# A decoder step on one Trainium2 core: the samples' attention moved into the first group's second gate-up stage of layer 0

## The chip, the core and the metric

The kernel runs on one core of one Trainium2 chip. A core has a matrix engine (TensorE, PE in the profile), a vector engine (VectorE, DVE), a scalar engine (ScalarE, ACT), a general engine (GpSimd, POOL) and a sync engine (SyncE, SP), which here issues all DMAs. The engines run their own instruction streams and meet at semaphores. The metric is device time in microseconds; lower is better.

## The reference

One inference step of a two-layer decoder for a prompt of 1024 tokens and for 8 samples of 8 new tokens each, with 512 cached positions per sample in pages. Layer 0 mixes by sparse attention (an indexer picks keys, then softmax attention over them) beside a pooling mixer; layer 1 by a gated spatial unit. Each layer ends in a SwiGLU feed-forward. Cut to the part that matters:

```python
def _dsa_block(q, iq, iw, qpos, k_all, v_all, ik_all, topk):
    rel = relu(einsum('bnhd,bsd->bnhs', iq, ik_all) * D_IDX ** -0.5)
    score = einsum('bnh,bnhs->bns', iw * N_IDX_HEADS ** -0.5, rel)     # masked to kpos <= qpos
    _, sel = lax.top_k(score, topk)
    k_sel, v_sel = take(k_all, sel), take(v_all, sel)
    logits = einsum('bnhgd,bnshd->bnhgs', qg, k_sel) * HEAD_DIM ** -0.5
    return einsum('bnhgs,bnshd->bnhgd', softmax(logits), v_sel)

def _swiglu(h, w_gu, w_down):
    gate, up = jnp.split(h @ w_gu, 2, axis=-1)
    return (jax.nn.silu(gate) * up) @ w_down

hs = hs + _rmsnorm(ms, norm_mix_post[layer])       # ms: mixer of the samples, with cached keys
hs = hs + _rmsnorm(_swiglu(_rmsnorm(hs, norm_ffn_pre[layer]), w_ffn_gate_up[layer], w_ffn_down[layer]), norm_ffn_post[layer])
```

## The kernel before, in words

The tokens are two groups: group 0 is prompt tokens 0 to 511, group 1 prompt tokens 512 to 1023 and the 64 sample tokens (width 576, done in two halves of 288). Activations stand transposed, eight blocks of 128 channels (`resid`, `mixed`). Every linear layer is cut into chunks of 128 output channels. Of a chunk, ACT makes the high part of the weights (`w_hi`), POOL the low part (`w_lo`), and PE does three products for each k-step (high by high, high by low, low by high). Two chunks are in flight, of the even chunks with PSUM banks 0 and 1, of the odd ones with 2 and 3. The feed-forward hidden size is done in two halves; one half is a gate-up stage (11 pairs of chunks, gate even and up odd, `Phase("gu", g, layer, half)`) and a down stage (`"dn"`).

The order of stages, written out by hand on each engine, is: input projections and indexers of both groups, attention of group 0, its output projection, gate-up and down of group 0 in layer 0 (halves 0 and 1), attention of group 1, the samples' attention (`attend_sample`), output projection of group 1, then layer 1 of group 0 and the rest. In the gate-up stages of group 0, DVE also does rounds of top-k for the large index tiles (`top_max`, `top_mark`), beside its two products (`TT` times the root, gate times up); ACT does `w_hi`, Silu and the copy to `hidden_split`; POOL does `w_lo`, one product and the low part of `hidden_split`.

The samples' attention in the kernel before: for each of eight samples PE transposes four pages of keys (line 1343), ACT copies them (1946), PE makes logits with the mask and the new keys (1375, 1376), DVE takes their minimum (2864), ACT the exponentials (1960), DVE divides (2866, 2869), PE transposes the probabilities (1350, 1351), ACT copies them (1951, 1952), PE multiplies with the values (1359, 1361). Everything has two buffers, and PE's order lets the steps of neighbouring samples overlap. SP loads the pages in four lots of eight (`key_value_pages`) during attention of group 1; then it loads back what was spilled: the residual of group 1 (`x_dram`), the residual and mixed rows of group 0 (`x0_dram`, `y0_dram`). These feed `hidden_update`, the end of group 0's layer 0, which runs under the output projection of group 1. SP's queue is in order: weights of the projection's chunks from 2 on are issued behind those loads.

Within the projection of group 1, six k-steps of chunk 0 are followed by a spread of the root (line 1075, `hidden_spread`), on which `hidden_update` waits.

## Time and profile before

| | us |
|---|---|
| median of 3 runs | 2657.81 (2653.18 to 2659.29) |
| the profiled execution | 2661.24 |
| its span | 2659.4 |
| PE busy in the span | 2541.2 (96%) |
| DVE / ACT / POOL busy | 1317.3 / 1027.7 / 1253.9 |

| stage (us of the span) | length |
|---|---|
| output projection, group 0 (412 to 456) | 43.6 |
| gate-up, group 0, layer 0, second half (652 to 772) | 119.8 |
| down behind it (772 to 832) | 60 |
| attention, group 1 (835 to 963) | 128 |
| samples' attention (963 to 999) | 36.6 |

PE is busy nearly all the time, so the chain that ends last is mostly PE's own; 79% of it is PE. A busy share does not say whether the matrix clock was full: that is the column PEclk, where 1.00 is 2.4 GHz and 0.50 is 1.2 GHz. A time line gives start and length of an instruction (or of a merged run of equal ones), and in brackets the idle time before it and who ended it. Ends of matmuls overlap the next starts, so lengths of steps are best taken from start to start.

### The profile page before, as it was taken

To read this page: it belongs to the slowest core of one execution; us is meant where nothing else is said; L and a number is where in the kernel's file an instruction comes from. 1 tells how busy PE (TensorE), PEld (TensorE's weight loads), DVE (VectorE), ACT (ScalarE), POOL (GpSimd) and SP (SyncE) were. 2 spreads that over 40 slices of the span, in tenths; PEclk is the share of its full clock that TensorE was granted. 3 is DMA by queue.
4 is the path that set the end of the run, shared out by engine and by line. 5 is a ranking of instruction groups with operands and counts; after the bars stand their busy time and mean duration, and the time that the engine had idled before them with its cause. 6 is when DMAs were issued, how large, how long until landed. Compare 5 with 4: busy or idle time off the path is not lost.

```text
span 2659.4 us, 42175 instructions
## 1 busy us (share of the span) xinstructions
PE 2541.2 (96%) x15118; PEld 2270.7 (85%) x15121; DVE 1317.3 (50%) x1705; ACT 1027.7 (39%) x1534; POOL 1253.9 (47%) x634
## 2 busy tenths in 40 slices
PE   6989869999998999999999999999999999999999
PEld 5779547888886769889999999888889999999999
DVE  4567777889877646554511233621344343220234
ACT  4545654422234645644422222532232435222222
POOL 4545243664665514535544443744543334443442
PEclk8989979999998999999999999999999999999999
DMA  6546012333333142332332232332343221232232
GB/s 154 129 105 154 16 60 64 103 104 93 95 105 113 43 146 68 123 104 87 112 92 70 83 86 72 96 105 85 95 134 119 72 81 43 86 89 75 81 94 68
DMA packets 451034, 246.41 MB, mean 93 GB/s; under 512 B 86668, under 2 KB 439648, under 8 KB 449383
## 3 DMA queue, kind: packets, MB, share of 16 engines
q1 hardware_dynamic: 450927, 244.99, 31.7%
q8 instruction: 66, 1.08, 0.2%
q14 instruction: 41, 0.34, 0.0%
HBM read 221.23 MB, written 23.82 MB: 92 GB/s over the span
## 4 chain that ended last, share of the span: by engine, by line
PE 79%; DVE 4%; ACT 3%; POOL 2%; issue 1%; DMA 1%; SPq 0%; DVEq 0%; POOLq 0%; ACTq 0%
PE psum L884 69%; PE psum L1306 1%; PE psum L1224 1%; PE psum L1328 1%; PE psum L1318 1%; POOL w_lo L2248 1%; DVE probs_t L2844 1%; PE psum L924 1%; PE psum L1049 1%; PE psum L1436 1%; ACT probs_t L1930 1%; PE psum L1075 0%; DVE row_stats L2830 0%; PE psum L1303 0%; DVE z_rows L3129 0%
## 5 line engine op out<-in xcount | busy, mean ns | idle before, releaser
L2248 POOL TENSOR_TENSOR w_lo<-w_raw,w_hi 128x1024 fp32r<-128x1024 f32 (+1 forms) x334 | 858.4, 2570 | 1133.8 <-ACT w_hi L1614 1115.0
L884 PE MATMUL psum<-act_split,w_hi 128*128 128x288 f32 (+1 forms) x5200 | 1049.6, 316 | 5.4 <-POOL w_lo L2248 5.3
L1614 ACT ACTIVATE w_hi<-w_raw 128x1024 fp32r<-128x1024 f32 (+1 forms) x332 | 372.9, 1123 | 1318.1 <-PE psum L884 1260.7
L884 PEld LDWEIGHTS psum<-act_split,w_hi 128*128 128x128 f32 x5200 | 808.2, 189 | 50.0 <-POOL w_lo L2248 5.8
L884 PE MATMUL psum<-act_split,w_lo 128*128 128x288 f32 (+1 forms) x2600 | 647.1, 315 | 0.0
L884 PE MATMUL psum<-hidden_split,w_hi 128*128 128x288 f32 (+1 forms) x2112 | 461.5, 327 | 0.5 <-POOL w_lo L2248 0.5
L884 PEld LDWEIGHTS psum<-act_split,w_lo 128*128 128x128 f32 x2600 | 433.7, 189 | 20.0
L884 PEld LDWEIGHTS psum<-hidden_split,w_hi 128*128 128x128 f32 x2112 | 339.4, 188 | 28.2 <-issue 0.9
L884 PE MATMUL psum<-act_split_first,w_hi 128*128 128x512 f32 x1088 | 340.1, 394 | 0.5 <-POOL w_lo L2248 0.3
L884 PE MATMUL psum<-hidden_split,w_lo 128*128 128x288 f32 (+1 forms) x1056 | 288.0, 327 | 0.0
L2964 DVE TENSOR_TENSOR temps<-psum,temps 128x512 f32<-128x512 f32 (+1 forms) x88 | 63.7, 724 | 358.5 <-PE psum L884 335.5
L884 PEld LDWEIGHTS psum<-act_split_first,w_hi 128*128 128x128 f32 x1088 | 203.6, 189 | 43.7 <-POOL w_lo L2248 1.1
L2956 DVE TENSOR_TENSOR temps<-psum,root_of_input 128x512 f32<-128x512 f32 (+1 forms) x88 | 63.7, 724 | 339.8 <-PE psum L884 332.2
L884 PE MATMUL psum<-act_split_first,w_lo 128*128 128x512 f32 x544 | 213.0, 392 | 0.0
L2478 DVE TENSOR_TENSOR square_sums<-square_sums,squares 128x512 f32<-128x512 f32 (+1 forms) x63 | 149.4, 2372 | 105.0 <-ACT squares L1979 60.9
L884 PEld LDWEIGHTS psum<-hidden_split,w_lo 128*128 128x128 f32 x1056 | 179.6, 188 | 13.8
L2967 DVE TENSOR_TENSOR hidden_split<-temps,hidden_split 128x576 f32 (+3 forms) x66 | 154.3, 2338 | 68.3 <-ACT hidden_split L1991 68.3
L2572 DVE MATCH_REPLACE8 scores<-top,scores 128x640 f32<-128x640 f32 (+3 forms) x192 | 170.0, 893 | 0.0
L2565 DVE MAX8 top<-scores 128x8 f32<-128x640 f32 (+3 forms) x192 | 164.7, 899 | 1.6
L2276 POOL TENSOR_TENSOR temps<-temps,root_of_input 128x512 f32<-128x512 f32 (+1 forms) x88 | 121.8, 1384 | 10.9 <-ACT temps L1988 10.9
L884 PEld LDWEIGHTS psum<-act_split_first,w_lo 128*128 128x128 f32 x544 | 102.7, 189 | 21.6
L1328 PE MATMUL psum<-probs_t,values_split 128*128 128x512 f32 x216 | 68.0, 425 | 17.8 <-DVE probs_t L2844 17.7
(334 smaller groups left out, 2452.9 us busy)
## 6 DMA issues: line engine op xcount, KB each, us to landing
w_raw<-in_w_ffn_gate_up SPq DMA_DIRECT2D x352, 256.0 KB, 3.2
w_raw<-in_w_ffn_down SPq DMA_DIRECT2D x64, 384.0 KB, 3.6
w_raw<-in_w_ffn_down SPq DMA_DIRECT2D x64, 320.0 KB, 4.0
w_raw<-in_w_in_odd SPq DMA_DIRECT2D x64, 256.0 KB, 3.0
w_raw<-in_w_in_even SPq DMA_DIRECT2D x60, 256.0 KB, 3.9
w_raw<-in_w_out_odd SPq DMA_DIRECT2D x32, 256.0 KB, 3.2
x_rows<-in_x_prompt SPq DMA_DIRECT2D x8, 512.0 KB, 6.0
w_raw<-in_w_out_even SPq DMA_DIRECT2D x32, 128.0 KB, 3.0
```

What stands on the lines that cost most here:

```text
L884: mm = pe.matmul(PS[:, 2 * p + b, 0:hi - lo], w[:, p, at], x(k)[:, lo:hi], start=(k == order[0] and w is WH and x is x_hi), stop=(k == ord ...
L924: mm = pe.matmul(PS[:, 2 * p + b, 0:hi - lo], w[:, p, at], x(k)[:, lo:hi], start=(k == 0 and w is WH and x is a_hi), stop=(k == ph.kt - 1 ...
L1328: mm = pe.matmul(PS[:, 6 + z, :], VS[:, v, kk, :], PT[:, kc % 2, q, :], start=kk == 0 and v == 0 and q == 0, stop=kk == t and v == 1)
L1614: act.activation(WH[:, p, 0:n], WR[:, p, 0:n], ACT.Copy).then_inc(S("w_hi"), 1)
L2248: pool.tensor_tensor(WL[:, p, 0:n], WR[:, p, 0:n], WH[:, p, 0:n].bitcast(F32), ALU.subtract).then_inc(S("w_lo"), 1)
L2276: pool.tensor_tensor(TT[:, 0, 0:T[g]], TT[:, 0, 0:T[g]], RB[g][:, 0:T[g]], ALU.mult).then_inc(S("gated"), 1)
L2478: dve.tensor_tensor(SS[:, 0:T[g]], SS[:, 0:T[g]], SQ[:, p, 0:T[g]], ALU.add).then_inc(S("ss_p"), 1)
L2565: ins_ = dve.max(M8[0:s.shape[0], m, :], s)
L2572: ins_ = dve.match_replace(out=s, in_to_replace=M8[0:s.shape[0], m, :], in_values=s, imm_value=CHOSEN)
L2956: dve.tensor_tensor(hv(TT[:, 0, 0:T[g]], g), lin(0, g), hv(RB[g][:, 0:T[g]], g), ALU.mult).then_inc(S("free_d0"), 1)
L2964: dve.tensor_tensor(hv(TT[:, 1, 0:T[g]], g), lin(1, g), hv(TT[:, 0, 0:T[g]], g), ALU.mult).then_inc(S("free_d1"), 1)
L2967: dve.tensor_tensor(flat(HR[:, 1, ds(i, 1), 0:T[g]]), TT[:, 1, 0:T[g]], flat(HR[:, 0, ds(i, 1), 0:T[g]].bitcast(F32)), ALU.subtract).then_ ...
```

## The change

The samples' attention leaves its place behind attention of group 1 and is done in pieces within gate-up of group 0, half 1, of layer 0. That stage is now written out (no loop) for its 22 chunks. Sample b has: transposes of its key pages in chunk 2b ahead of k-step 4, logits in chunk 2b+1 ahead of k-step 4, transposes of the probabilities in chunk 2b+3 ahead of k-step 3, values in chunk 2b+4 ahead of k-step 6. ACT's and DVE's parts follow their own work for a chunk (`sample_aside`, `sample_guest`). Key copy, probabilities and their transposes have one buffer instead of two; transposed keys and transposed probabilities share PSUM bank 6, logits use banks 4 and 5, the outputs bank 7. The pages lie where the residual `X` was (it is spilled then), and SP issues the four pages of keys and values of sample b between the weights of that stage. The queries of the samples are loaded in the first attention; the mask is made by DVE ahead of the first down stage, the heads are laid out by ACT behind it. The loads of spilled rows change place: the residual and six of eight mixed blocks of group 0 once the last prompt logits are made, the last two mixed blocks and the residual of group 1 once the last prompt values are done.

```diff
-        XH = over("resid_spare", [P, NB, T[0]], F32, h_at, 4096)
-        YH = over("mixed_spare", [P, NB, T[0]], F32, h_at, 8192)
-        SQH = over("squares_spare", [P, 2, T[0]], F32, h_at, 0)
+        XH = over("resid_spare", [P, NB, T[0]], F32, h_at, 0)
+        YH = over("mixed_spare", [P, 6, T[0]], F32, h_at, 9600)
+        YT = over("mixed_spare_tail", [P, 2, T[0]], F32, h_at, 7168)
+        SQH = over("squares_spare", [P, 2, T[0]], F32, h_at, 4096)
...
+        KP = over("key_pages", [P, 2, NPG, P], F32, x_at, 0)
+        VP = over("value_pages", [P, 4, NPG, P], F32, x_at, 1024)
+        KTB = over("page_keys_t", [P, PAST], F32, x_at, 3072)
+        PTS = over("probs_sample_t", [P, 5 * NS], F32, x_at, 3584)
+        PRS = over("probs_sample", [NS, KCOL], F32, x_at, 3904)
+        QZ = over("queries_sample", [P, DB, NS], F32, ikt_at, 0)
+        MKS = over("mask_sample", [NS, KCOL], BF16, ikt_at, 512)
+        QS = over("queries_sample_rows", [P, 4, NS], F32, ikt_at, 800)
...
+            def pages(b):
+
+                if b > 1:
+                    sp.wait_ge(S("kt_ps"), b - 1)
+                if b > 3:
+                    sp.wait_ge(S("pvs_mm"), b - 3)
+                for i in range(NPG):
+                    page = sp.value_load(PGT[0:1, NPG * b + i:NPG * b + i + 1], min_val=0, max_val=DB * NPG * 5 // 4 - 1)
+                    for to, name in ((KP[:, b % 2, i, :], "cache_k"), (VP[:, b % 4, i, :], "cache_v")):
+                        rows = ins[name][0].rearrange("n s h d -> n s (h d)")[ds(page, 1)].rearrange("a s d -> (a s) d")
+                        sp.dma_start(to, rows).then_inc(S(f"pages_in{b % 2}"), 16)
...
+                    sp.dma_start(QS[:], q_dram[1, :, :, 512:T[1]]).then_inc(S("qs_in"), 16)
...
                     next_queries(g, k)
                 if g:
-                    key_value_pages(0)
-                    sp.wait_ge(S("mk"), 6)
-                    key_value_pages(1)
-                    sp.wait_ge(S("qst_lo"), 16)
-                    sp.dma_start(QR[:, :, 0:NS], q_dram[1, :, :, 512:T[1]]).then_inc(S("q_in"), 16)
-                    key_value_pages(2)
-                    sp.wait_ge(S("p_tr"), kbase(7, 1))
-                    key_value_pages(3)
-                    sp.wait_ge(S("p_tr"), kbase(8, 0))
-                    sp.dma_start(X[:], x_dram).then_inc(S("first_in"), 16)
+                    sp.wait_ge(S("qk_mm"), 64)
+                    sp.dma_start(XH[:], x0_dram).then_inc(S("first_in"), 16)
+                    sp.dma_start(YH[:], y0_dram[:, 0:6, :]).then_inc(S("first_in"), 16)
                     sp.wait_ge(S("pv_mm"), kbase(8, 0))
-                    sp.dma_start(XH[:], x0_dram).then_inc(S("first_in"), 16)
-                    sp.wait_ge(S("pvs_mm"), 2)
-                    sp.dma_start(YH[:], y0_dram).then_inc(S("first_in"), 16)
+                    sp.dma_start(YT[:], y0_dram[:, 6:8, :]).then_inc(S("tail_in"), 16)
+                    sp.dma_start(X[:], x_dram).then_inc(S("second_in"), 16)
...
-            channel(0, 0, (1,))
+            ph = phase("gu", 0, 0, 1)
+            head(ph)
+            pages(0)
+            for i in range(1, FH):
+                some(ph, i, i + 1)
+                if i < DB:
+                    pages(i)
+            head(phase("dn", 0, 0, 1))
+            rest(phase("dn", 0, 0, 1))
...
+            def sample_keys(b):
+                pe.wait_ge(S(f"pages_in{b % 2}"), 128 * (b // 2 + 1))
+                wait(pe, S("ktb"), b)
+                wait(pe, S("pts"), b - 1)
+                for j in range(NPG):
+                    mm = pe.transpose(PS[:, 6, P * j:P * j + P], KP[:, b % 2, j, :], IDENT)
+                mm.then_inc(S("kt_ps"), 1)
+
+            def sample_logits(b):
+                pe.wait_ge(S("ktb"), b + 1)
+                pe.wait_ge(S("iqz"), 3)
+                pe.wait_ge(S("qz0"), 3)
+                wait(pe, S("exps"), b)
+                for bank, lo, hi, keys in ((4, 0, PAST, KTB[:]), (5, PAST, KCOL, KT[:, SEQ:SEQ + NS])):
+                    pe.matmul(PS[0:NS, bank, 0:hi - lo], EB[:, b, :], MKS[:, lo:hi], start=True, stop=False)
+                    mm = pe.matmul(PS[0:NS, bank, 0:hi - lo], QZ[:, b, :], keys, start=False, stop=True)
+                mm.then_inc(S("qks_mm"), 1)
+
+            def sample_turn(b):
+                pe.wait_ge(S("ps_norm"), 2 * b + 2)
+                pe.wait_ge(S("ktb"), min(b + 2, DB))
+                wait(pe, S("pts"), b)
+                for j in range(NPG):
+                    pe.transpose(PS[:, 6, NS * j:NS * j + NS], PRS[:, P * j:P * j + P], IDENT[0:NS, 0:NS])
+                pe.transpose(PS[0:NS, 6, NS * NPG:NS * NPG + NS], PRS[:, PAST:KCOL], IDENT[0:NS, 0:NS]).then_inc(S("ps_tr"), 1)
+
+            def sample_values(b):
+                pe.wait_ge(S("pts"), b + 1)
+                for j in range(NPG):
+                    pe.matmul(PS[:, 7, NS * b:NS * b + NS], VP[:, b % 4, j, :], PTS[:, NS * j:NS * j + NS],
+                              start=j == 0, stop=False)
+                pe.matmul(PS[:, 7, NS * b:NS * b + NS], VN[0:NS, 8, :], PTS[0:NS, NS * NPG:NS * NPG + NS],
+                          start=False, stop=True).then_inc(S("pvs_mm"), 1)
...
-            gate_up(phase("gu", 0, 0, 1))
+            sample = {}
+            for b in range(DB):
+                sample[2 * b, 4] = lambda b=b: sample_keys(b)
+                sample[2 * b + 1, 4] = lambda b=b: sample_logits(b)
+                sample[2 * b + 3, 3] = lambda b=b: sample_turn(b)
+                sample[2 * b + 4, 6] = lambda b=b: sample_values(b)
+            gate_up(phase("gu", 0, 0, 1), sample, FH)
             down(phase("dn", 0, 0, 1))
             attend(1)
-            attend_sample()
...
+            def page_keys(b):
+                act.wait_ge(S("kt_ps"), b + 1)
+                wait(act, S("qks_mm"), b)
+                act.activation(KTB[:], PS[:, 6, :], ACT.Copy).then_inc(S("ktb"), 1)
+
+            def sample_turned(b):
+                act.wait_ge(S("ps_tr"), b + 1)
+                wait(act, S("pvs_mm"), b)
+                act.activation(PTS[:, 0:NS * NPG], PS[:, 6, 0:NS * NPG], ACT.Copy)
+                act.activation(PTS[0:NS, NS * NPG:NS * NPG + NS], PS[0:NS, 6, NS * NPG:NS * NPG + NS], ACT.Copy).then_inc(S("pts"), 1)
+
+            def sample_exponentials(b):
+                act.wait_ge(S("mxs"), b + 1)
+                wait(act, S("ps_tr"), b)
+                act.activation(PRS[:], PSF[0:NS, 2048:2048 + KCOL], ACT.Exp,
+                               bias=MX[0:NS, 0, b:b + 1], scale=-1.0, accum_out=MX[0:NS, 2, b:b + 1]).then_inc(S("exps"), 1)
+
+            def sample_aside(c):
+                b, odd = divmod(c, 2)
+                if odd == 0 and b < DB:
+                    page_keys(b)
+                if odd and 1 <= b <= DB:
+                    sample_turned(b - 1)
+                if odd and b < DB:
+                    sample_exponentials(b)
...
-            gate_up(phase("gu", 0, 0, 1))
+            for j in range(4):
+                heads_of_sample(j)
+            gate_up(phase("gu", 0, 0, 1), False, sample_aside, FH)
...
+            def sample_mask():
+
+                dve.memset(QZ[:], 0.0).then_inc(S("qz0"), 1)
+                dve.wait_ge(S("top"), 2 * (SMALL + 17))
+                dve.tensor_scalar(MKS[:], SCS[:, 0:KCOL], SPLITTER, MASK, ALU.is_gt, ALU.mult).then_inc(S("qz0"), 1)
+
+            def sample_guest(c):
+                b, odd = divmod(c, 2)
+                if odd and b < DB:
                     dve.wait_ge(S("qks_mm"), b + 1)
-                    dve.tensor_reduce(MX[0:NS, 0, b:b + 1], PSF[0:NS, 1024 * (b % 2):1024 * (b % 2) + KCOL], AX.X, ALU.min).then_inc(S("mx"), 1)
+                    dve.tensor_reduce(MX[0:NS, 0, b:b + 1], PSF[0:NS, 2048:2048 + KCOL], AX.X, ALU.min).then_inc(S("mxs"), 1)
+                if odd == 0 and 1 <= b <= DB:
+                    b -= 1
                     dve.wait_ge(S("exps"), b + 1)
-                    dve.reciprocal(MX[0:NS, 3, b:b + 1], MX[0:NS, 2, b:b + 1]).then_inc(S("inv"), 1)
-                    dve.wait_ge(S("inv"), 64 + b + 1)
-                    pr = PRS[:, b % 2, :]
-                    dve.tensor_scalar(pr, pr, MX[0:NS, 3, b:b + 1], None, ALU.mult).then_inc(S("ps_norm"), 1)
-                dve.wait_ge(S("o_hi"), 17)
-                for half in range(2):
-                    r = slice(64 * half, 64 * half + 64)
-                    for j in range(4):
-                        at = AR[r, 0, j, 512:T[1]].rearrange("p (b t) -> p b t", b=DB)
-                        lo = AR[r, 1, j, 512:T[1]].rearrange("p (b t) -> p b t", b=DB)
-                        ins_ = dve.tensor_tensor(lo, PS[r, 7, :].rearrange("p (b h t) -> p h b t", b=DB, h=8)[:, 4 * half + j],
-                                                 at.bitcast(F32), ALU.subtract)
-                ins_.then_inc(S("o_lo"), 1)
+                    dve.reciprocal(MX[0:NS, 3, b:b + 1], MX[0:NS, 2, b:b + 1]).then_inc(S("ps_norm"), 1)
+                    dve.wait_ge(S("ps_norm"), 2 * b + 1)
+                    dve.tensor_scalar(PRS[:], PRS[:], MX[0:NS, 3, b:b + 1], None, ALU.mult).then_inc(S("ps_norm"), 1)
...
                     if (g, s) == (1, 0):
-                        dve.wait_ge(S("first_in"), 48)
+                        dve.wait_ge(S("second_in"), 16)
                     if (g, s) == (0, 1):
-                        dve.wait_ge(S("first_in"), 48)
+                        dve.wait_ge(S("first_in"), 32)
                     if (g, s) == (0, 2):
-                        dve.wait_ge(S("first_in"), 80)
+                        dve.wait_ge(S("first_in"), 64)
                 else:
                     dve.wait_ge(S("x_new"), m + n)
+                    if (g, s) == (0, 1) and n == 6:
+                        dve.wait_ge(S("tail_in"), 16)
...
             gate_up(phase("gu", 0, 0, 0), BIG0)
+            sample_mask()
             down(phase("dn", 0, 0, 0), 1, (2, 2, 2, 1), BIG0 + FH)
-            gate_up(phase("gu", 0, 0, 1), BIG0 + FH + 7)
+            gate_up(phase("gu", 0, 0, 1), BIG0 + FH + 7, None, sample_guest)
```

On PE, inside that gate-up stage: before, a chunk is a loop's body of products only.

```order
L1004 UNCONDITIONAL_BRANCH
L1004 ISA
L876 REGISTER_ALU
L884 MATMUL psum<-act_split,w_hi 128x512 x2
L884 MATMUL psum<-act_split,w_lo 128x512
L884 MATMUL psum<-act_split,w_hi 128x512 x2
```

After (chunk 3: the end of its k-step 2, then the probabilities of sample 0, k-step 3, the logits of sample 1, k-step 4):

```order
L888 MATMUL psum<-act_split,w_hi 128x512 x2
L888 MATMUL psum<-act_split,w_lo 128x512
L1363 MATMUL psum<-constants,probs_sample 128x64 x4
L1364 MATMUL psum<-constants,probs_sample 64x64
L888 MATMUL psum<-act_split,w_hi 128x512 x2
L888 MATMUL psum<-act_split,w_lo 128x512
L1354 MATMUL psum<-mask_sample,spread_bf_78 64x512
L1355 MATMUL psum<-page_keys_t,queries_sample 64x512
L1354 MATMUL psum<-mask_sample,spread_bf_78 64x64
L1355 MATMUL psum<-keys_t,queries_sample 64x64
L888 MATMUL psum<-act_split,w_hi 128x512 x2
L888 MATMUL psum<-act_split,w_lo 128x512
```

The small products of two samples now stand between k-steps of one chunk.

On ACT, in the same stage, the loop's body before:

```order
L1614 ACTIVATE w_hi<-w_raw 128x1024
L173 REGISTER_ALU
L1988 ACTIVATE temps<-temps 128x512
L173 REGISTER_ALU
L1614 ACTIVATE w_hi<-w_raw 128x1024
L1991 ISA
L1991 ACTIVATE hidden_split<-temps 128x512
```

After (from the end of chunk 1, where sample 0's exponentials are, over chunk 2 to chunk 3):

```order
L1984 ACTIVATE hidden_split<-temps 128x512
L1946 ACT_TABLE_LOAD
L1946 ACTIVATE probs_sample,row_stats<-psum,row_stats 64x576
L1607 ACTIVATE w_hi<-w_raw 128x1024
L1981 ACT_TABLE_LOAD
L1981 ACTIVATE temps<-temps 128x512
L1935 ACTIVATE page_keys_t<-psum 128x512
L1607 ACTIVATE w_hi<-w_raw 128x1024
L1984 ACTIVATE hidden_split<-temps 128x512
L1940 ACTIVATE probs_sample_t<-psum 128x256
L1941 ACTIVATE probs_sample_t<-psum 64x64
```

Keys' copies, probabilities' copies and exponentials have come in, and a table load stands ahead of each exponential and ahead of the Silu (`temps<-temps`) behind it.

On SP, at the end of attention of group 1, before (the last page of keys and values, the spilled rows, then the projection's weights):

```order
L676 DMA key_pages_139<-in_cache_k 128x128
L676 REGISTER_ALU
L676 DMA value_pages_140<-in_cache_v 128x128
L672 REGISTER_ALU
L672 COMPARE_AND_BRANCH
L711 DMA resid<-resid_spill 128x4608
L713 DMA resid_spare<-resid_spill_first 128x4096
L715 DMA mixed_spare<-mixed_spill_first 128x4096
L585 UNCONDITIONAL_BRANCH
L585 ISA
L536 ISA
L536 DMA w_raw<-in_w_out_even 64x4x128
```

After:

```order
L702 DMA act_split<-pool_spill 128x2304
L692 DMA queries_tile<-queries_spill 128x4x128 x2
L707 DMA resid_spare<-resid_spill_first 128x4096
L708 DMA mixed_spare<-mixed_spill_first 128x3072
L710 DMA mixed_spare_tail<-mixed_spill_first 128x1024
L711 DMA resid<-resid_spill 128x4608
L584 UNCONDITIONAL_BRANCH
L584 ISA
L535 ISA
L535 DMA w_raw<-in_w_out_even 64x4x128
```

The pages are gone from here, and the residual stands last ahead of the weights.

## Rows read from the trace of the kernel before

**Rows 1.** Windows: us, busy of PE, PEld, DVE, ACT, POOL, PEclk, DMA.
```profile
412.25:455.80 43.55, 43.55 (x196) 36.04 (x194) 36.55 (x57) 14.94 (x22) 16.79 (x7) 1.00 0.27 76
652.40:772.20 119.80, 119.80 (x530) 99.26 (x529) 96.51 (x148) 35.18 (x45) 79.55 (x43) 1.00 0.32 95
962.60:999.20 36.60, 34.73 (x201) 22.59 (x199) 12.00 (x25) 15.42 (x41) 0.00 (x0) 0.92 0.63 213
```

**Rows 2.** PE's timeline (start us, us, what): samples' attention, then the projection.
```profile
962.63 1.03 PE L1343 MATMUL psum<-constants,key_pages 128*128 128x128 f32 x8
...
972.86 0.66 PE L1343 MATMUL psum<-constants,key_pages 128*128 128x128 f32 x4
...
976.88 0.66 PE L1343 MATMUL psum<-constants,key_pages 128*128 128x128 f32 x4
...
999.24 1.33 PE L884 MATMUL psum<-act_split,w_hi 128*128 128x288 f32 x4
...
1005.98 1.06 PE L1075 MATMUL psum<-constants,root_rstd 128*128 128x128 f32 x8
```

**Rows 3.** PE's timeline: chunk 1 and its k-step 3 in gate-up.
```profile
657.85 0.61 PE L884 MATMUL psum<-act_split,w_hi 128*128 128x512 f32 x2
...
659.89 0.62 PE L884 MATMUL psum<-act_split,w_hi 128*128 128x512 f32 x2
```

**Rows 4.** ACT's timeline behind chunk 0 of gate-up.
```profile
658.24 1.06 ACT L1614 ACTIVATE w_hi<-w_raw 128x1024 fp32r<-128x1024 f32 x1 [4.00 <-PE psum L884]
659.20 0.61 ACT L1988 ACTIVATE temps<-temps 128x512 f32<-128x512 f32 x1
```

**Rows 5.** ACT's timeline in layer 1: table load between w_hi and Gelu.
```profile
1133.90 1.06 ACT L1614 ACTIVATE w_hi<-w_raw 128x1024 fp32r<-128x1024 f32 x1 [1.21 <-PE psum L884]
1134.98 1.28 ACT L2134 ACT_TABLE_LOAD   x1
1136.27 0.63 ACT L2134 ACTIVATE u_t<-u_t 128x512 f32<-128x512 f32 x1
```

**Rows 6.** ACT's timeline: keys' copy; w_hi of the projection's chunk 2.
```profile
973.55 0.60 ACT L1946 ACTIVATE page_keys_t<-psum 128x512 f32<-128x512 f32 x1
...
1012.17 1.04 ACT L1614 ACTIVATE w_hi<-w_raw 128x1024 fp32r<-128x1024 f32 x1
```

**Rows 7.** PE's timeline: gaps inside dense work and what follows.
```profile
1217.62 1.06 PE L1014 MATMUL psum<-constants,square_sums 128*128 128x1 f32 x8 [1.08 <-DVE square_sums L2885]
1218.54 1.31 PE L884 MATMUL psum<-act_split,w_hi 128*128 128x288 f32 x4
...
1222.51 0.69 PE L884 MATMUL psum<-act_split,w_hi 128*128 128x288 f32 x4
...
2110.27 1.16 PE L1436 MATMUL psum<-w_spatial_t,z_rows 128*128 128x128 f32 x8 [1.99 <-DVE z_rows L3129]
...
2111.72 0.80 PE L884 MATMUL psum<-act_split,w_hi 128*128 128x288 f32 x4
...
2112.61 0.69 PE L884 MATMUL psum<-act_split,w_hi 128*128 128x288 f32 x4
...
2113.40 0.69 PE L884 MATMUL psum<-act_split,w_hi 128*128 128x288 f32 x4
```

**Rows 8.** Window behind the gap at 1217; columns as in rows 1.
```profile
1219.00:1220.00 1.00, 1.00 (x6) 1.00 (x6) 0.10 (x1) 1.00 (x1) 0.00 (x0) 0.50 1.13 337
```

**Rows 9.** SP's timeline: two page issues of the old stage.
```profile
897.75 0.36 SPq L676 DMA_DIRECT2D key_pages<-in_cache_k  x1
...
899.77 0.36 SPq L676 DMA_DIRECT2D key_pages<-in_cache_k  x1
```

**Rows 10.** The DMA view: what, count, KB each, median us to landing.
```profile
resid<-resid_spill SPq DMA_DIRECT2D x1, 2304.0 KB, 9.4
...
w_raw<-in_w_out_even SPq DMA_DIRECT2D x16, 256.0 KB, 3.1
```

**Rows 11.** PE's timeline: chunk 2 of the projection starts.
```profile
1015.77 0.80 PE L884 MATMUL psum<-act_split,w_hi 128*128 128x288 f32 x4 [0.75 <-POOL w_lo L2248]
```

166 lines of the change are left out of this document (46 added, 120 removed).

## The prediction

> **What bounds the kernel now.** I read the windows by stage first. In the stage that takes the moved work, 652.4 to 772.2 us, PE is busy all of the 119.8 us while DVE is busy 96.5, POOL 79.6 and ACT 35.2 [rows 1]: TensorE alone sets the pace. In the samples' attention, 962.6 to 999.2, PE is busy 34.7 of 36.6 us, with ACT at 15.4 and DVE at 12.0 [rows 1]. So the work that is moved is itself TensorE work, and it goes to a stage where TensorE has no room. The move can win only what is not PE's work: the start and end of the old stage, and whatever the low clock cost there. Next I read PE's own timeline for the sizes, then ACT's, because PE will wait for ACT in the new place.
>
> **What is removed.** The old stage starts at 962.63 and the output projection behind it at 999.24 [rows 2]: 36.6 us leave the path. The projection then ran its first six k-steps in 1005.98 - 999.24 = 6.74 us [rows 2]. A k-step of this width takes 2113.40 - 2112.61 = 0.79 at full clock [rows 7], six take 4.8. In the new kernel the projection follows the prompt's attention directly. The same succession exists already in the first group, whose projection runs at a granted clock of 1.00 throughout, 412 to 456 us [rows 1]. I therefore take 6.74 - 4.8 = 1.9 us more as won. Together -38.5 us.
>
> **What PE gets in gate-up.** One sample costs PE 976.88 - 972.86 = 4.02 us in the old steady state (page transposes, logits, probability transposes, values) [rows 2]; eight are 32.2 us. They stand in 32 groups (turn of keys, logits, turn of probabilities, values) between wide products, and the first wide pair behind small ones starts late: between 0 and 0.1 us each, since a k-step right behind small products takes 2112.61 - 2111.72 = 0.89 where the usual one takes 0.79 [rows 7]. I take near half, 1.4 us for 32: +33.6, bounds 32.2 and 35.4.
>
> **The wait that PE gets.** PS bank 6 holds in turn the transposed keys and the transposed probabilities. So the turn of sample b's probabilities, in chunk 2b+3 ahead of k-step 3, waits for ACT's copy of the keys of sample b+1, which ACT makes behind chunk 2b+2. Count from the start of chunk 2b+3. PE is at k-step 3 after 659.89 - 657.85 = 2.04 us [rows 3]. ACT starts w_hi at 658.24 - 657.85 = 0.39, and Silu at 1.35 [rows 4]. In the changed kernel Exp and Silu alternate on ACT, and the order shows an ACT_TABLE_LOAD ahead of every Exp and of every Silu behind one, 16 in all; none stands in this stage before. Where such a load stands between w_hi and its function, it starts 1134.98 - 1133.90 = 1.08 after w_hi starts and the function 1136.27 - 1134.98 = 1.29 later [rows 5]. So: w_hi 0.39, load 1.47, Silu 2.76, keys' copy about 0.52 later (instructions on ACT overlap by some 0.1) at 3.28, its 0.60 [rows 6] to 3.88, PE some 0.1 later: 3.98. PE waits 3.98 - 2.04 = 1.94 us. This holds for b = 0 to 6 (for b = 7 there is no next key copy): 7 x 1.94 = +13.6 us. Without the loads it would be 0.5 each. Queued behind the waiting turn is all of PE's remaining chunk; nothing hides it. The Exp's own load falls behind an odd chunk, whose followers are due a whole chunk later, and costs nothing.
>
> The Trainium skill, "ScalarE: Activation LUTs", section "Table sets: the hidden batching unit", says to batch calls by table set, which speaks against this change. Its section "What ACT_TABLE_LOAD costs" puts a switch at 1.28 us plus 1.38 of drain. The rows show 1.28 and no drain: w_hi ends at 1134.96, the load starts at 1134.98 [rows 5]. By the page the wait would be 3.3 us and the sum about 9.7 us more.
>
> **What the wait does to the clock.** In the linear stages the trace has four gaps of PE of 1.08 to 1.99 us inside dense work (the shortest and the longest stand; the other two are of the same kind) [rows 7]. Behind three of them, the shortest among these, the granted clock is 0.50, the 1.2 GHz level, for some 3.5 us, as in 1219 to 1220 [rows 8]; behind the longest the k-steps still come at 0.79. A fall costs 1222.51 - 1218.54 = 3.97 for three k-steps of 0.79, so 1.6 us [rows 7]. Three in four of seven gaps is five: +8.0 us, bounds 0 and 11.2. The small products right behind each gap are why I don't go lower.
>
> **The other engines.** DVE gets at most the old stage's 12.0 us [rows 1] on 96.5 in a stage that grows past 160 us; its scaling of the probabilities is queued before the long top-k instructions and is done before ACT's copy. ACT gets 15.4 + 16 x 1.28 = 36 on 35.2, again far from full; POOL gets nothing. They cost nothing because PE's own work covers them; were DVE late, PE's turn would wait for it instead. SP issues four pages a sample at 899.77 - 897.75 = 2.0 us each [rows 9], 8 us within a period of 15, ahead of weights that are due a chunk and more later: taken as 0, bound +1 us. The queries' small load in the first attention and the mask made ahead of the down stage: 0, as DVE has several us there before its next product.
>
> **The projection's weights.** The residual (2304 KB) and two blocks of the mixed rows (512 KB) are now issued at about 962.9, when the attention that ended at 962.63 [rows 2] has its last values, and the weights of chunk 2 behind them; before, the whole samples' stage lay between the loads and their use. The residual takes 9.4 us to land [rows 10]; 512 KB more are between 0 and 2.1 us by its rate, I take 1.2; then the weights, between 0 and the 3.1 of their own row [rows 10], I take 1.5: 962.9 + 9.4 + 1.2 + 1.5 = 975.0. ACT would want them 1012.17 - 1005.98 = 6.2 us after the spread starts [rows 2, 6], in the new kernel at 962.63 + 4.8 + 6.2 = 973.6. So about 1.4 us late, 1.7 with the delay of the issue itself, on top of the 0.75 that PE waits there anyway [rows 11]: +1.7, bounds 0 and 5 (with a fall of the clock behind it). The loads of the first group's residual and most of its mixed rows are issued after the last logits product and have the last value rounds to land in: 0. Taking the heads' copies out of the last rounds of attention gains 0 to 0.5; I take 0.
>
> **Sum.** -38.5 + 33.6 + 13.6 + 8.0 + 1.7 = +18.4 us on the profiled execution of 2661.24. The median of the runs shown is 3.4 lower, 2657.81, so 2676.2 us (0.7% slower). With the bounds: +7.6 (no fall, no late start, weights 0.3 late) to +26.7, 2665 to 2685.
>
> **Rivals.**
> 1. *PE does not wait, or hardly.* If the key copy comes in time (the load overlapped with PE's chunk in a way that the rows don't show), neither wait nor fall of the clock arises: -38.5 + 33.6 + 1.7 = -3.2, 2654.6, and 2651.5 with the lowest bounds. It is on the other side. The point is whether the copy ends within 2.04 us of the chunk's start; for it only that the loads carry no wait of their own, against it that ACT executes in order and has w_hi, load, Silu ahead. 0.15, of which 0.06 below -0.2%.
> 2. *A load costs more than its row*, as the skill's page has it; worked with a further stop as long as w_hi (1.06) ahead of each load, 7 x 1.06 = 7.4 us more, 2684. 0.06.
> 3. *Pages or weights come late.* If SP's page issues push the weights of gate-up past their use, each pair of chunks loses a few tenths to 1 us, 8 in all, 2684; for it that SP is in order, against it that eight page issues take 8 us of each 15 and the weights' own issues 1 to 2. 0.05.
> 4. *The clock stays low through the stage's middle*, because gap, turn and logits follow closely: every chunk then costs twice 5.44; two such chunks more are 11 us, 2687 and up. 0.06.
> The forecast's own case keeps 0.68. That the work is not moved is excluded by the order.
>
> **How the numbers follow.** A measurement of this kernel tells about 0.2%, 5.3 us, from no change. Slower by more: 0.68 + 0.06 + 0.05 + 0.06 less a little where the forecast's gaps are short, 0.82. Within: 0.11. Faster: 0.07. The range 2662 to 2686 holds the forecast's bounds and most of rivals 2 and 3, and leaves out rival 1 and the far end of 4.
>
> **What would show it.** In gate-up: eight periods of about 17 us for two chunks, seven PE gaps near 1.9 us at the turn of probabilities released by ACT's page_keys_t, table loads of 1.28 between w_hi and Silu, clock 0.5 behind most gaps, the stage 170 to 178 us long. In the projection: clock 1.00 and one gap of 2 to 3 us for w_lo at chunk 2. I am wrong if the gaps are half a microsecond, or if the clock holds.

## The result and the profile after

| | before | after |
|---|---|---|
| median of 6 runs each, us | 2657.97 (2652.08 to 2659.38) | 2671.56 (2666.58 to 2672.73) |
| profiled execution / its span, us | 2661.24 / 2659.4 | 2672.57 / 2670.8 |

The changed kernel is slower: ratio 1.0054, 95% interval 1.0040 to 1.0067, 13.6 us between the medians and 11.3 between the profiled executions. The forecast had +18.4, 2676.2 in a range of 2662 to 2686. Direction and mechanism of the wait hold; the size is 4.6 us too large.

First the windows by stage of the kernel after. Columns as in rows 1: length, busy time of PE, PEld, DVE, ACT and POOL, the granted clock, the DMA share, GB/s.

```profile
653.20:822.10 168.90, 157.87 (x729) 118.94 (x729) 107.90 (x180) 73.17 (x117) 78.97 (x43) 0.99 0.32 92
677.00:678.00 1.00, 1.00 (x3) 0.52 (x2) 0.77 (x1) 0.00 (x0) 0.57 (x1) 0.50 0.25 63
...
1012.10:1070.50 58.40, 55.85 (x410) 55.37 (x409) 38.11 (x35) 31.38 (x50) 29.67 (x15) 0.97 0.44 131
```

The first row answers to the second of rows 1: the gate-up stage has grown from 119.8 to 168.9 us, and PE is busy in 157.9 of them. So 11 us of the growth is PE standing still, which it never did in this stage before. The second row is one microsecond with the clock at 0.50; the third is the projection of group 1.

The length of each part of the span, from the first product of one stage to the first of the next:

| part | before | after | difference | forecast |
|---|---|---|---|---|
| up to gate-up (group 0, layer 0, second half) | 652.41 | 653.25 | +0.8 | 0 |
| gate-up with the samples' groups | 119.68 | 168.92 | +49.2 | +55.2 |
| down, attention of group 1, (before) samples' attention | 227.15 | 190.01 | -37.1 | -36.6 |
| projection of group 1 | 57.46 | 58.36 | +0.9 | -0.2 |
| from there to the end | 1602.7 | 1600.3 | -2.4 | 0 |

I don't put the last line and the first down to the change. The last part takes 1596.8 to 1604.1 us in the traces of all kernels below, and 1600.3 and 1604.1 in two executions of the same changed kernel. Some of it is the clock: the kernel before has stretches of 0.50 at 1218 and at 1648 (some 1.7 us lost in each) that the kernel after lacks, but the kernel after has one at 1076 and one at 2124 that the kernel before lacks.

PE's timeline after, the first product of each of the eight turns of the probabilities; in brackets the idle time before it and what ended it:

```profile
676.39 0.43 PE L1363 MATMUL psum<-constants,probs_sample 64*128 64x64 f32 x4 [1.63 <-ACT page_keys_t L1935]
...
694.94 0.43 PE L1363 MATMUL psum<-constants,probs_sample 64*128 64x64 f32 x4 [1.57 <-issue]
...
711.96 0.43 PE L1363 MATMUL psum<-constants,probs_sample 64*128 64x64 f32 x4 [1.57 <-issue]
...
728.99 0.43 PE L1363 MATMUL psum<-constants,probs_sample 64*128 64x64 f32 x4 [1.57 <-issue]
...
794.97 0.46 PE L1363 MATMUL psum<-constants,probs_sample 64*128 64x64 f32 x4
```

Seven gaps, one for each sample but the last, 17.02 us from turn to turn (711.96 to 728.99); only the first period has 18.55, since a fall of the clock lies in it. "issue" in the later rows says that the profile names no releaser. The start of PE's chunk ahead of the second turn and, in a fence of its own, ACT's timeline of the same moment do:

```profile
691.15 0.62 PE L888 MATMUL psum<-act_split,w_hi 128*128 128x512 f32 x2
```

```profile
691.35 1.06 ACT L1607 ACTIVATE w_hi<-w_raw 128x1024 fp32r<-128x1024 f32 x1 [3.23 <-PE psum L888]
692.43 1.28 ACT L1981 ACT_TABLE_LOAD   x1
693.73 0.63 ACT L1981 ACTIVATE temps<-temps 128x512 f32<-128x512 f32 x1
694.26 0.58 ACT L1935 ACTIVATE page_keys_t<-psum 128x512 f32<-128x512 f32 x1
```

The copy of the keys ends at 694.84 and the turn starts at 694.94. It is the chain of the forecast (w_hi, load, Silu, copy), 0.2 us shorter: ACT starts w_hi 0.20 behind the start of PE's chunk, not 0.39 as in rows 3 and 4.

### The profile page after: what moved, and what is told of

It is laid out like the page before. It is cut to its first block, busy times and chain, and to the rows that moved or that the text cites. A ratio compares the mean times of both kernels' runs of the same rounds, so it can differ in the third digit from the quotient of the medians.

```text
span 2670.8 us, 41648 instructions
## 1 busy us (share of the span) xinstructions
PE 2540.8 (95%) x15118; PEld 2264.0 (85%) x15121; DVE 1314.1 (49%) x1705; ACT 1049.2 (39%) x1550; POOL 1253.3 (47%) x634
## 3 DMA queue, kind: packets, MB, share of 16 engines
q8 instruction: 70, 1.15, 0.2%
## 4 chain that ended last, share of the span: by engine, by line
PE 80%; DVE 4%; ACT 3%; issue 2%; POOL 1%; DMA 1%; SPq 0%; DVEq 0%; POOLq 0%; ACTq 0%
PE psum L888 70%; PE psum L1232 1%; PE psum L1336 1%; PE psum L1314 1%; DVE probs_t L2839 1%; PE psum L1326 1%; PE psum L928 1%; PE psum L1057 1%; ACT probs_t L1923 1%; PE psum L1425 1%; PE psum L1083 0%; DVE row_stats L2825 0%; DVE z_rows L3136 0%; PE psum L1355 0%; POOL w_lo L2243 0%
## 5 line engine op out<-in xcount | busy, mean ns | idle before, releaser
L2972 DVE TENSOR_TENSOR hidden_split<-temps,hidden_split 128x576 f32 (+3 forms) x66 | 154.4, 2339 | 68.4 <-ACT hidden_split L1984 68.4
```

Of the source, the lines that this page charges most:

```text
L2972: dve.tensor_tensor(flat(HR[:, 1, ds(i, 1), 0:T[g]]), TT[:, 1, 0:T[g]], flat(HR[:, 0, ds(i, 1), 0:T[g]].bitcast(F32)), ALU.subtract).then_ ...
```

## The experiments

All but the first two rows are edits of the changed kernel; `after again` is its file unchanged. Stage times are read as in the table above, from each run's own trace; the ratio is to the kernel before on the same chip, of which the median was 2657.8 to 2658.5.

| kernel | gate-up | projection | span | median | ratio (95%) |
|---|---|---|---|---|---|
| before | 119.7 | 57.5 | 2659.4 | 2658.0 | 1 |
| after | 168.9 | 58.4 | 2670.8 | 2671.6 | 1.0054 (1.0040 to 1.0067) |
| turn later | 156.1 | 57.1 | 2656.7 | 2661.0 | 1.0013 (1.0004 to 1.0022) |
| copy first | 156.1 | 56.6 | 2655.3 | 2656.7 | 1.0001 (0.9991 to 1.0011) |
| no switch | 157.4 | 56.4 | 2657.3 | 2660.7 | 1.0008 (0.9998 to 1.0017) |
| weights first | 168.9 | 55.5 | 2665.1 | 2667.5 | 1.0044 (1.0030 to 1.0057) |
| copy and weights | 156.1 | 55.5 | 2652.5 | 2655.6 | 0.9991 (0.9982 to 1.0001) |
| merged | 154.4 | 55.5 | 2658.3 | 2654.6 | 0.9990 (0.9979 to 1.0000) |
| turn early | 186.7 | 58.5 | 2688.1 | 2689.9, one run | |
| after again | 168.9 | 58.0 | 2673.6 | 2675.4, one run | |
| samples left out | 120.6 | 60.9 | 2625.3 | 2626.3 | 0.9885 (0.9865 to 0.9904) |

### The turn later

```diff
-                sample[2 * b + 1, 4] = lambda b=b: sample_logits(b)
-                sample[2 * b + 3, 3] = lambda b=b: sample_turn(b)
+                sample[2 * b + 1, 7] = lambda b=b: sample_logits(b)
+                sample[2 * b + 3, 6] = lambda b=b: sample_turn(b)
```

> The turn of the probabilities stands ahead of k-step 6 in place of 3 and the logits ahead of k-step 7 in place of 4; all else is the changed kernel. In the changed kernel TensorE waits 1.6 us (1.73 with what follows) ahead of seven turns for ScalarE's copy of the page keys. Theory (the copy comes 3.8 us behind the end of the chunk, three k-steps of 0.68 more cover it): no gap for page_keys_t in the trace, a period of two chunks of 15.3 us in place of 17.02, the stage 168.9 - 7 x 1.73 = 156.8 us, 155.1 if the one fall of the clock in it goes too; the time 2671.6 - 12.1 to - 13.8 = 2657.8 to 2659.5, no different from the kernel before. Rival (the gap only stands where another wait would stand: DVE's minimum, ScalarE's exponentials or the weights are as late): the gap moves to values, keys or weights, the period stays above 16.5 and the time above 2667.

The window of its gate-up stage:

```profile
656.10:812.20 156.10, 156.10 (x730) 118.63 (x729) 107.93 (x180) 73.13 (x117) 79.30 (x43) 1.00 0.34 100
```

PE is busy in all of the 156.1 us; no gap has taken the place of the seven. ACT does the same work as in the kernel after (73.1 us, 16 loads), so the loads are not a cost in themselves: they cost where they stand ahead of something that PE needs at once. The median of 2661.0 is above the 2659.5 that the theory allowed, and why is open: there are stage times of one execution only, and that one took 2658.5. It reaches gate-up at 656.18, 3.8 us later than the kernel before; between 273 and 294 its granted clock is 0.50 nearly throughout (mean 0.51, against 0.76 in the kernel before). The change does not reach that part, and executions differ there. The window there of this kernel, then of the kernel before:

```profile
273.00:294.00 21.00, 15.07 (x68) 11.91 (x68) 9.95 (x18) 9.16 (x19) 3.21 (x2) 0.51 0.14 35
```

```profile
273.00:294.00 21.00, 14.44 (x81) 10.35 (x82) 12.62 (x20) 10.15 (x21) 3.20 (x2) 0.76 0.13 33
```

### The copy first

```diff
                     for p in (0, 1):
+                        if aside == sample_aside and p == 0 and i < DB:
+                            page_keys(i)
                         wait(act, S("w_used"), ph.c0 + 2 * i + p + 1)
...
-                if odd == 0 and b < DB:
-                    page_keys(b)
```

> Only the place of ScalarE's copy of the page keys is changed: ahead of the split of the weights that follows the even chunk, not behind the Silu of that chunk; the turn stays ahead of k-step 3. Theory (what TensorE waits for is the row ahead of the copy: w_hi 1.06, table load 1.28, Silu 0.63): the copy is done by the chunk's end or 0.6 us behind it, the seven gaps are gone although the turn has not moved, Silu and what hangs on it come up to 0.6 us later with no wait on TensorE; stage 155 to 157 us, time 2658 to 2660. Rival (w_hi, now 0.6 later, or the later Silu holds the next chunks): a gap of 0.3 to 0.6 us for w_lo or for the bank of the gate shows in each period, stage 159 to 162 us, time 2662 to 2665.

PE's window, the start of a chunk and its turns, then ACT's timeline of a period:

```profile
652.60:808.70 156.10, 156.10 (x729) 118.63 (x728) 107.92 (x180) 73.07 (x117) 79.03 (x43) 1.00 0.34 99
```

```profile
702.76 0.62 PE L888 MATMUL psum<-act_split,w_hi 128*128 128x512 f32 x2
...
704.91 0.46 PE L1363 MATMUL psum<-constants,probs_sample 64*128 64x64 f32 x4
...
720.33 0.46 PE L1363 MATMUL psum<-constants,probs_sample 64*128 64x64 f32 x4
...
735.74 0.46 PE L1363 MATMUL psum<-constants,probs_sample 64*128 64x64 f32 x4
```

```profile
699.63 0.58 ACT L1937 ACTIVATE page_keys_t<-psum 128x512 f32<-128x512 f32 x1
702.96 1.06 ACT L1607 ACTIVATE w_hi<-w_raw 128x1024 fp32r<-128x1024 f32 x1 [2.75 <-PE psum L888]
704.04 1.28 ACT L1981 ACT_TABLE_LOAD   x1
705.33 0.64 ACT L1981 ACTIVATE temps<-temps 128x512 f32<-128x512 f32 x1
```

The turn stands where it stood and no longer waits. The copy now runs at 699.63 in time in which ACT used to idle, long before the chunk ends, and w_hi is not even later. The period is 15.41. All 16 table loads are still there, so the wait hangs on where the copy stands in ACT's order, and moving it gives back 12.8 us of the stage (168.9 to 156.1), 1.5 of them the fall of the clock. It also gives the two other terms without wait or fall: of the 17.02 in the kernel after, 1.61 are the wait (7 x 1.61 = 11.3 us), and the groups cost 156.10 - 119.68 = 36.4 us, 4.55 a sample. PE gets to the turn 704.91 - 702.76 = 2.15 us after its chunk's start, where rows 3 had 2.04.

### No switch

```diff
-                act.activation(PRS[:], PSF[0:NS, 2048:2048 + KCOL], ACT.Exp,
+                act.activation(PRS[:], PSF[0:NS, 2048:2048 + KCOL], ACT.Silu,
```

> The samples' exponentials are replaced by Silu of the same numbers (that part of the result is changed), so no table is loaded in the stage; every instruction keeps its place. Theory (a load lies in front of the copy with its row, 1.28 us, and nothing more): the seven gaps shrink from 1.6 to about 0.3 us, the stage to 168.9 - 7 x 1.28 = 159.9 us, the time to 2662.6, and 2661 without the fall of the clock. Rival A (a load costs its row and a drain of about as much again): the gaps vanish altogether and with them all 12.1 us, time 2659.5 or less. Rival B (the loads are hidden beside ScalarE's waits for VectorE and TensorE): the gaps stay above 1 us, time above 2667.

PE's first turns, and ACT ahead of the third:

```profile
674.95 0.43 PE L1363 MATMUL psum<-constants,probs_sample 64*128 64x64 f32 x4 [0.21 <-ACT page_keys_t L1935]
...
690.55 0.43 PE L1363 MATMUL psum<-constants,probs_sample 64*128 64x64 f32 x4
...
706.14 0.43 PE L1363 MATMUL psum<-constants,probs_sample 64*128 64x64 f32 x4
```

```profile
703.98 1.06 ACT L1607 ACTIVATE w_hi<-w_raw 128x1024 fp32r<-128x1024 f32 x1 [4.66 <-PE psum L888]
704.95 0.62 ACT L1981 ACTIVATE temps<-temps 128x512 f32<-128x512 f32 x1
705.47 0.58 ACT L1935 ACTIVATE page_keys_t<-psum 128x512 f32<-128x512 f32 x1
```

The period falls from 17.02 to 15.59, so a load on the way costs 1.43, and 0.18 of wait stays (15.59 - 15.41). Its row is 1.28. The rest is overlap that it takes away, as ACT's starts say: w_hi to Silu is 704.95 - 703.98 = 0.97 here, and 693.73 - 691.35 = 2.38 with the load, 1.41 more. That is between the theory (1.28) and rival A (which wanted all of it gone), near the theory. The Trainium skill, "ScalarE: Activation LUTs", section "What ACT_TABLE_LOAD costs", has 1.28 us plus 1.38 of drain: the runs here show the first and a tenth of the second. The same page's section "Table sets: the hidden batching unit" advises to batch calls by table set. A stage without any load is the most that this could give: 11.5 us here (168.9 to 157.4), 1.5 of them the fall of the clock. The order of one copy is worth more, 12.8, with all loads in place.

### The weights first

```diff
                     sp.dma_start(YH[:], y0_dram[:, 0:6, :]).then_inc(S("first_in"), 16)
+                    some(phase("out", 1), 1, 2)
                     sp.wait_ge(S("pv_mm"), kbase(8, 0))
...
-            rest(phase("out", 1))
+            rest(phase("out", 1), 2)
```

> SyncE issues the output projection's chunks 2 and 3 ahead of its wait for the last values and so ahead of the loads of the mixed activations' tail and of the second group's residual; all else is the changed kernel. Theory (in the changed kernel these weights queue behind a residual load of 2304 KB that lands 9.5 us after its issue; TensorE waits 2.1 us for w_lo at chunk 2 and loses 1.7 us more to a clock of 0.5 behind it): both go, the projection's stage 58.4 - 3.8 = 54.6 us, the time 2667.8. Rival (the wait was for the split on ScalarE, which stands behind the samples' last copies and the root, not for the load): the gap at chunk 2 stays at 2 us and the time at 2671. A second rival: the residual, now issued later, holds VectorE at the sum behind the projection; then the gain is lost in the stage behind it.

Chunk 2 of the projection on PE, of the kernel after and then of this one:

```profile
1028.10 0.98 PE L888 MATMUL psum<-act_split,w_hi 128*128 128x288 f32 x4 [2.11 <-POOL w_lo L2243]
```

```profile
1024.99 0.79 PE L889 MATMUL psum<-act_split,w_hi 128*128 128x288 f32 x4 [0.76 <-POOL w_lo L2244]
```

In the kernel after, ACT's w_hi of that chunk waits for the weights themselves, which it did not before [rows 6]:

```profile
1024.56 1.06 ACT L1607 ACTIVATE w_hi<-w_raw 128x1024 fp32r<-128x1024 f32 x1 [1.29 <-DMA w_raw<-in_w_out_even]
```

The gap is back at the 0.75 of rows 11, and the 1.7 us at a clock of 0.50 behind it (1028 to 1032 in the kernel after) are gone: 58.4 to 55.5 us, and the median 2667.5 for the 2667.8 expected. So the first rival, that the split on ScalarE was what came late, is excluded too. The stage was expected at 54.6: that left out the 0.76 that ACT and POOL need in any case. The second rival is excluded, since the part behind the projection is no longer (1599.2 us, against 1600.3).

How late the weights come goes with the load in front of them. The kernels with this order of loads, in rising time of the residual's 2304 KB to landing, are no switch 9.2, after again 9.2, copy first 9.3, after 9.5, turn later and turn early 9.6 us; PE waits 1.7, 1.8, 1.8, 2.1, 2.3 and 2.3 us. Only three of these six waits (after, after again, turn early) have a fall of the clock behind them, so the projection is 56.4 to 58.5 us long, and this mend is worth between 1 and 3 us.

### Both mends

The two diffs above together.

> Both mends together on the changed kernel: ScalarE copies the page keys ahead of the split of the weights, and SyncE issues the projection's chunks 2 and 3 ahead of the last loads. If they add up: gate-up stage 156.1 us as with the copy first alone, projection 55.5 as with the weights first alone (56.6 with the copy first alone, which had no fall of the clock in the projection), so 1.1 us less than the 2656.7 of the copy first alone: 2655.6, a ratio of 0.9990 to 1.0000 to the kernel before (2657.8). If they don't add up (the time that the projection gains is lost in front of it or behind it): 2656.7 or more, ratio 1.000.

They add up: 156.1 and 55.5 us, and the median is 2655.6 as expected. The 1.1 us from the copy first alone to this one are below what the medians can show; the stage times carry it.

### Four groups in two places

```diff
-            for b in range(DB):
-                sample[2 * b, 4] = lambda b=b: sample_keys(b)
-                sample[2 * b + 1, 4] = lambda b=b: sample_logits(b)
-                sample[2 * b + 3, 3] = lambda b=b: sample_turn(b)
-                sample[2 * b + 4, 6] = lambda b=b: sample_values(b)
+            for b in range(DB + 2):
+                sample[2 * b, 6] = lambda b=b: (sample_keys(b) if b < DB else None, sample_values(b - 2) if b > 1 else None)
+                sample[2 * b + 1, 6] = lambda b=b: (sample_turn(b - 1) if 0 < b <= DB else None, sample_logits(b) if b < DB else None)
```

> As the kernel with both mends, and the samples' four groups in a period of two chunks are put into two places: keys of one sample with the values of another ahead of k-step 6 of the even chunk, turn with logits ahead of k-step 6 of the odd one. Theory (of the 4.53 us that the groups cost in a period, 0.51 more than the forecast had from the old stage, each of the four entries into the chunk costs about 0.1 on the k-step behind it and up to 0.1 ahead of it): the period falls from 15.41 to about 15.2, the stage from 156.1 to 154.3 to 154.7 us. Rival (the extra 0.51 is in the groups' own matmuls, which run slower beside ScalarE and VectorE than in the old stage): the period stays at 15.41, the stage at 156.1. A second rival: the group in one piece is long enough (2.3 us) for something else to be late, a wait for the page keys or a fall of the clock in the stage.

PE's turns; this kernel has both mends too:

```profile
710.77 0.46 PE L1364 MATMUL psum<-constants,probs_sample 64*128 64x64 f32 x4
...
725.94 0.46 PE L1364 MATMUL psum<-constants,probs_sample 64*128 64x64 f32 x4
...
741.11 0.46 PE L1364 MATMUL psum<-constants,probs_sample 64*128 64x64 f32 x4
```

The period is 15.17, 0.24 less, for two entries less: 0.12 each. The stage is 154.4 us. If the other two entries cost as much, four in a period make about 0.5, which is the difference between the 4.02 of the old stage and the 4.53 here (15.41 less two chunks of 5.44). The forecast bounded an entry by 0 and 0.1 and took near half. The span of the profiled execution, 2658.3, is no shorter, since this execution reached gate-up only at 656.96 (before: 652.41). By the median this is the fastest of the complete kernels here, 17 us below the kernel after; its ratio to the kernel before, 0.9990, is within the 0.2% that I count as no change.

### The turn early

```diff
-                sample[2 * b + 3, 3] = lambda b=b: sample_turn(b)
+                sample[2 * b + 3, 1] = lambda b=b: sample_turn(b)
```

> The turn stands ahead of k-step 1 in place of 3, all else is the changed kernel: TensorE gets to it 2 x 0.68 = 1.36 us sooner and the copy it waits for comes when it did, so seven gaps of about 1.6 + 1.4 = 3.0 us. What it tells is the clock: the changed kernel had one fall of the clock behind seven gaps of 1.6 us, where the forecast had five. Theory (how long the gap is decides it): with gaps of 3.0 us most of the seven are followed by a granted clock of 0.50, 1.7 us each; stage 168.9 + 9.5 - 1.7 + 5 to 7 x 1.7 = 185 to 189 us. Rival (it's the first gap of a stage that meets it, whatever its length, or chance): one fall or none, stage 176.7 to 178.4 us.

PE's timeline at six of the turns:

```profile
674.41 0.66 PE L1363 MATMUL psum<-constants,probs_sample 64*128 64x64 f32 x4 [2.99 <-ACT page_keys_t L1935]
...
695.64 0.43 PE L1363 MATMUL psum<-constants,probs_sample 64*128 64x64 f32 x4 [2.93 <-issue]
...
714.03 0.43 PE L1363 MATMUL psum<-constants,probs_sample 64*128 64x64 f32 x4 [2.92 <-issue]
...
733.94 0.43 PE L1363 MATMUL psum<-constants,probs_sample 64*128 64x64 f32 x4 [2.93 <-issue]
...
753.86 0.43 PE L1363 MATMUL psum<-constants,probs_sample 64*128 64x64 f32 x4 [2.92 <-issue]
...
772.28 0.43 PE L1363 MATMUL psum<-constants,probs_sample 64*128 64x64 f32 x4 [2.93 <-issue]
```

A period without a fall is 18.39 (695.64 to 714.03), or 15.41 and the wait of 2.98. Periods of 19.91 (714.03 to 733.94) have a stretch at half clock in them, and the first, 21.23, has two. Behind five of the seven gaps the clock falls, and the stage is 186.7 us: inside the 185 to 189 of the theory and far from the 178.4 of the rival, by one execution. The windows of two such places, and then of the one fall in the repeat of the kernel after (next part):

```profile
673.00:681.00 8.00, 6.59 (x17) 3.77 (x17) 2.80 (x3) 1.26 (x3) 2.57 (x2) 0.57 0.38 109
714.00:719.00 5.00, 4.97 (x16) 3.16 (x17) 1.46 (x2) 0.00 (x0) 1.23 (x2) 0.66 0.45 131
```

```profile
744.00:748.00 4.00, 4.00 (x11) 1.43 (x11) 1.38 (x2) 0.00 (x0) 1.16 (x1) 0.57 0.56 164
```

### The kernel after once more

The same file.

> The changed kernel once more, for the falls of the clock from execution to execution. Theory (a fall behind a gap of 1.6 us is a matter of chance, with perhaps 1 in 7): the number of falls in the stage differs from one, 0 to 3, and the stage is 167.2 us and 1.7 more for each. Rival (the fall belongs to the first of the gaps, which is the same in every execution): again one fall, right behind the first gap, stage 168.9 us.

Again one fall, but behind the fifth gap (744) and not behind the first (677). In the trace of the weights first, whose gate-up is also that of the kernel after, it is the seventh (777). Three executions, 21 gaps of 1.6 us, three falls, one in each. The rival that it belongs to the first gap is wrong, and the theory of mere chance is not shown either: it expected the number to differ, and it was one each time. How the chip comes to one fall in seven such gaps stays open.

Two gaps of rows 7 stand in every kernel here, in code that no edit touches, so the eleven traces can be read for them too. Behind the 1.08 us ahead of `square_sums` the clock falls in ten of eleven executions; the kernel after is the exception. Behind the 1.99 or 2.00 us ahead of `z_rows` it falls in eight of eleven; the kernel before is one of the exceptions. The kernel after behind both, then the kernel before behind the second:

```profile
1232.60:1236.00 3.40, 3.40 (x27) 3.40 (x28) 0.18 (x1) 1.66 (x3) 0.00 (x0) 1.00 0.54 159
2124.30:2127.30 3.00, 3.00 (x15) 3.00 (x14) 0.78 (x2) 0.78 (x1) 0.00 (x0) 0.50 0.00 0
```

```profile
2110.30:2113.30 3.00, 3.00 (x22) 2.81 (x23) 0.00 (x0) 0.00 (x0) 0.00 (x0) 1.00 0.10 28
```

So the same gap in the same code comes with and without a fall, and a gap of 1.08 there has it far more often than one of 1.6 in gate-up.

### The samples left out

```diff
-            for b in range(DB):
...
-                sample[2 * b + 4, 6] = lambda b=b: sample_values(b)
+            sample[2 * DB + 2, 6] = lambda: pe.matmul(PS[:, 7, :], IDENT, KT[:, 0:512], start=True, stop=True).then_inc(S("pvs_mm"), 1)
```

> The samples' attention is left out of the changed kernel: its page loads, its matmuls, ScalarE's copies and exponentials and VectorE's minimum and scaling; one matmul of 512 columns stands in for its result. It is the kernel that both kernels have in common, so it prices the two places. Theory (the stages read from the traces are all there is): the stage is that of the kernel before and 0.4 to 1 us for the one matmul, 120.1 to 120.7 us, 48.2 to 48.8 less than in the changed kernel, and nothing is given back elsewhere; time 2671.6 - 48.5 = 2623.1, which puts the old place at 2657.8 - 2623.1 = 34.7 us (forecast 36.6 less 1.9 of low clock behind it). Rival (part of what the stage gives up is taken back, because the pages' loads or the load on ScalarE cover something else): stage above 122 us or time above 2627. Rival the other way (the pages slow the weights' loads elsewhere): time below 2621.

This kernel leaves out the samples' attention, so their result is missing from its output. The stage is 120.6 as expected; the time is not 2623.1 but 2626.3. In the trace 2.5 us more than in the kernel after stand in the projection (60.9). Its chunk 2 on PE, the window behind it, ACT's w_hi of that chunk, and the DMA view's row of the residual, in a fence each:

```profile
980.51 1.33 PE L884 MATMUL psum<-act_split,w_hi 128*128 128x288 f32 x4 [3.44 <-POOL w_lo L2229]
```

```profile
980.00:986.00 6.00, 5.49 (x23) 5.49 (x24) 5.96 (x5) 4.86 (x8) 5.84 (x4) 0.50 0.31 87
```

```profile
976.98 1.06 ACT L1599 ACTIVATE w_hi<-w_raw 128x1024 fp32r<-128x1024 f32 x1 [2.66 <-DMA w_raw<-in_w_out_even]
```

```profile
resid<-resid_spill SPq DMA_DIRECT2D x1, 2304.0 KB, 11.0
```

The same residual load took 11.0 us here and 9.5 in the kernel after, and ACT's wait for the weights behind it is longer by nearly as much (2.66 and 1.29), PE's by 1.3. The other 1.2 us are clock: behind the gap it stays at 0.50 to 986.4, for 5.9 us of matmuls, and in the kernel after to 1032, for under 4. So the expectation that nothing changes outside the stage was wrong by these 2.5 us. A 2304 KB load in front of weights that are due at once makes the projection depend on how long that load takes; why it took 11.0 here is open. By the medians the old place of the samples' attention costs 2658.1 - 2626.3 = 31.8 us and the new one 45.3, with this projection in the base of both.

## Why the prediction was right, and where it was off

**What bounds the stage: right.** PE was full in gate-up, and without waits the moved work costs 36.4 us there for 36.6 taken out of its old place. The move was worth nothing even before the waits: the kernel with the copy first is at a ratio of 1.0001.

**What is removed: -38.5 forecast.** The part from down to the projection is 37.1 shorter, 36.6 forecast; the stretches at 0.50 in attention are also 3.4 us shorter than before (17.1 and 20.5), worth at most 1.7 us, so the term agrees within about 1 us and not better. The projection starts at full clock, as forecast (-1.9): its only stretch at 0.50 is the one behind the wait for w_lo.

**The groups on PE: +33.6 forecast, 36.4 measured.** The term was mis-sized, and 1.0 beyond its own upper bound of 35.4. The bound of 0.1 for an entry came from one narrow k-step behind a gap [rows 7]; an entry measures 0.12, by the merged groups, which leaves a sample's matmuls at 4.05, as good as the 4.02 of the old place.

**The waits: +13.6 forecast, 11.3 measured.** Right in place, number (seven) and chain, which two independent edits confirm: take the copy out from behind Silu, or bring the turn later, and they go. Each is 1.61, not 1.94. Two starts in the chain were mis-sized, both read in the first chunks of the old stage. ACT starts w_hi 0.20 behind the chunk's start in the steady period, not 0.39, and PE is at the turn after 2.15 us, not 2.04. The load with its lost overlap was right (1.41 measured, 1.29 and 0.12 of start in the forecast).

**The clock: +8.0 forecast, 1.5 measured.** This is the step that failed, by 6.5 us: the rate of "three in four" was carried from four gaps in other stages of one execution into this one. In gate-up gaps of 1.6 us were followed by a fall once in seven, in each of three executions, and gaps of 2.9 us five times in seven. At the two old places that stand in every kernel here the rate was about right (18 of 22), so it was the carrying over that was wrong and not only a small sample. Its bounds, 0 to 11.2, hold the value, but one of the forecast's own signs of being wrong, that the clock holds, came behind six gaps of seven.

**The projection's weights: +1.7 forecast; 1.35 measured** by the wait (2.11 for 0.75), and 1.7 more of low clock behind it, which the forecast had only in its upper bound. Together with the -1.9 that is +1.15, and the stage is +0.9.

**The other engines: right.** DVE is busy 107.9 of 168.9 us, ACT 73.2 with its 16 loads, POOL 79.0; PE waits for none of them in that stage but for ACT's copy, seven times.

The sum with the measured terms: -37.1 + 36.4 + 11.3 + 1.5 + 0.9 = +13.0, and +0.8 and -2.4 from parts that the change does not reach make the 11.4 of the spans. The misses of terms were in both directions (+2.8 for the groups, -2.3 for the waits, -6.5 for the clock). Set against the spans, the +18.4 is 7.0 too large. That the time came within 4.6 us is in part luck: the profiled execution of the kernel before stood 3.3 us above its median and that of the kernel after only 1.0, so the medians lie 13.6 apart and the spans 11.4.

**The rivals.** The first (PE hardly waits) would have given 2654.6; it is what the kernel with the copy first does, at 2656.7, 2.1 above. The second (a load costs more than its row) is excluded by no switch: 0.15 more, not 1.06. The third is excluded in gate-up, where no wait for pages or weights shows. The fourth shows nowhere.
